# Order of the gate steps, transposes, copies and exponentials in the attention loop of a decoder layer

## What is computed

```
hn   = rmsnorm(x)
proj = hn @ w_in                      # q, k, v of two mixers, 3 head gates, and mg (2 x 1024 columns)
o_a  = banded_attention(window 128, 8 heads, sinks, bias)            # branch A
o_cmp, o_slc = compressed (63 blocks) and full causal attention      # branches C and S
o_win = banded_attention(window 512, 8 heads, bias)                  # branch W
o_b  = g0 * o_cmp + g1 * o_slc + g2 * o_win
g_a, g_b = sigmoid(mg)
h = x + (g_a * (o_a @ w_br_a) + g_b * (o_b @ w_br_b)) @ w_out
h = h + moe(rmsnorm(h))               # 32 experts, top-1 group, top-2 in it
out = rmsnorm(h)
```

## Time and profile before

| what | value |
|---|---|
| time, median of 3 runs | 1778.69 us (1776.9 to 1779.84) |
| the profiled execution, its own time | 1784.23 us |
| its span | 1782.4 us |
| granted clock over the span | 0.954 |
| PE busy | 1557.8 us (87%) |
| DVE busy | 537.1 us (30%) |
| ACT busy | 348.3 us (20%) |
| POOL busy | 262.8 us (15%) |

### The profile page before, as it was taken

How to read it: one execution, slowest core, us unless ns; L and a number is a source line. 1 busy time by engine, 2 the same in 40 slices (tenths; PEclk the granted TensorE clock), 3 DMA queues, 4 the chain that set the end, 5 groups by cost and what they waited for, 6 DMA issues and landing times.

```text
span 1782.4 us, 20856 instructions
## 1 busy us (share of the span) xinstructions
PE 1557.8 (87%) x7526; PEld 828.0 (46%) x7527; DVE 537.1 (30%) x1378; ACT 348.3 (20%) x859; POOL 262.8 (15%) x363
## 2 busy tenths in 40 slices
PE   6999998989989898988999994199799999889990
PEld 3554543434444444443444552156355666446650
DVE  4210005665565545553222215011011111101116
ACT  3000003343433433342000111011011111111112
POOL 2000002333232232221000000300000000000003
PEclk9999999999999999998999997599899999999995
DMA  9124602443111111002536410979999999999967
GB/s 254 26 59 57 132 0 100 166 142 95 30 33 34 30 24 42 25 18 77 204 115 232 172 53 18 341 283 380 383 389 384 379 391 381 391 390 383 381 223 283
DMA packets 130215, 334.21 MB, mean 188 GB/s; under 512 B 36792, under 2 KB 72664, under 8 KB 120944
## 3 DMA queue, kind: packets, MB, share of 16 engines
q1 hardware_dynamic: 112208, 291.88, 46.8%
q0 software_dynamic: 9552, 29.55, 5.0%
q10 hardware_dynamic: 8400, 12.07, 1.9%
HBM read 276.06 MB, written 57.41 MB: 187 GB/s over the span
## 4 chain that ended last, share of the span: by engine, by line
PE 71%; DMA 9%; DVE 8%; SPq 6%; issue 3%; ACT 2%; POOL 2%; ACTq 0%; POOLq 0%; DVEq 0%
PE PS L741 13%; PE PS L642 10%; PE PS L531 10%; PE PS L755 7%; PE PS L704 6%; PE PS L673 5%; SPq L301 5%; PE PS L628 4%; PE PS L589 4%; PE PS L608 3%; PE PS L526 2%; DMA BA<-w 2%; DMA WA<-w 2%; DMA BA<-rows_d 2%; DVE mx L1022 1%
## 5 line engine op out<-in xcount | busy, mean ns | idle before, releaser
L642 PE MATMUL PS<-WA 128*128 128x512 f32 x512 | 260.3, 621 | 17.8 <-ACT WA L833 17.8
L741 PE MATMUL PS<-WA,BA 128*64 128x256 f32 x2048 | 235.8, 388 | 14.1 <-DMA WA<-w 12.9
L741 PEld LDWEIGHTS PS<-WA,BA 128*64 128x64 f32 x2048 | 172.9, 140 | 84.6 <-issue 22.1
L531 PE MATMUL PS<-WA,BA 128*128 128x512 f32 x416 | 183.1, 601 | 5.1 <-DVE WA L937 5.1
L1248 POOL TENSOR_SCALAR BA<-BA,rin,gates 128x640 f32<-128x640 f32 (+7 forms) x128 | 99.8, 780 | 301.8 <-DVE rin L1045 301.7
L1161 DVE SCALAR_TENSOR_TENSOR BA<-BA,PS 128x256 f32<-128x256 f32 x46 | 19.4, 421 | 408.4 <-ACT BA L880 408.4
L642 PEld LDWEIGHTS PS<-WA 128*128 128x128 f32 x512 | 85.6, 191 | 111.5 <-issue 80.9
L826 ACT ACTIVATE BA<-PS,ngm 128x640 f32<-128x640 f32 (+7 forms) x128 | 89.7, 701 | 218.2 <-DVE ngm L1023 218.0
L531 PEld LDWEIGHTS PS<-WA,BA 128*128 128x128 f32 x416 | 79.6, 193 | 103.9 <-issue 98.3
L755 PE MATMUL PS<-WA,BA 128*64 128x512 f32 x512 | 116.9, 597 | 11.7 <-DVE BA L1171 7.6
L1287 POOL DMA_DIRECT2D BA<-rows_d x92 | 48.1, 522 | 531.1 <-PE PS L722 528.1
(11 more groups left out here) (207 smaller groups left out, 1361.4 us busy)
## 6 DMA issues: line engine op xcount, KB each, us to landing
WA<-w SPq DMA_DIRECT2D x66, 2048.0 KB, 34.4
BA<-w SPq DMA_DIRECT2D x30, 2048.0 KB, 36.7
rows_d<-WA SPq DMA_DIRECT2D x7, 2048.0 KB, 7.5
BA<-rows_d POOLq DMA_DIRECT2D x94, 128.0 KB, 7.2
rows_d<-BA ACTq DMA_DIRECT2D x92, 128.0 KB, 7.8
WA<-w_in SPq DMA_DIRECT2D x16, 512.0 KB, 5.5
gates_d<-WA SPq DMA_DIRECT2D x32, 256.0 KB, 2.2
WA<-gates_d SPq DMA_DIRECT2D x8, 1024.0 KB, 6.0
```

The source lines that it names most:

```text
L531: mm = pe.matmul(PS[:, j % 4, :], ws[:, c % 6, k, :], hnT[:, k, 512 * h:512 * h + 512], start=(k == 0), stop=(k == KT - 1))
L642: mm = pe.matmul(PS[:, 6, :], gw[:, j, k, :], hnT[:, k, 512 * hf:512 * hf + 512], start=(k == 0), stop=(k == KT - 1))
L741: mm = pe.matmul(PS[DH * h:DH * h + DH, bank, 0:256], xT[:, k, :], w[par][:, k, 256 * h:256 * h + 256], start=(k == 0), stop=(k == KT - 1))
```

## The change

On PE the transposes and the values of a turn of the loop now come directly behind its scores, and its gate steps behind those. On ACT a turn with a trailing unit keeps the order exponential, copies; in a turn with a leading unit (A and C among them) the copies of n - 2 come ahead of the exponential. The tanh of a gate tile is the last thing of a turn, behind the move of the sums. No instruction is added or removed; DVE, POOL and SP keep their orders. The lines in the changed kernel are moved by 3 on PE (L608 is L611, L642 is L645) and otherwise on ACT.

```diff
+    def leads(n):
+        return units[n][1] in "AC" or units[n][2] < REP
...
         for n in range(NU + 3):
             if n < NU:
-                if units[n][1] in "AC" or units[n][2] < REP:
+                if leads(n):
                     scores(n)
-                for step in steps_at[n]:
-                    gate_step(step)
             if 2 <= n < NU + 2:
                 turn(n - 2)
             if n >= 3 and (n - 3) == last_of[units[n - 3][:2]]:
                 values(*units[n - 3][:2])
+            if n < NU:
+                for step in steps_at[n]:
+                    gate_step(step)
...
         for n in range(NU + 3):
-            if n < NU:
-                i, br, h, kbs = units[n]
-                ...
-                last.then_inc(S["exp_done"], 1)
-                for m in tile_done_at.get(n, ()):
-                    ...
+            if n < NU and not leads(n):
+                exponential(n)
             if 2 <= n < NU + 2:
-                for m in range(first_group[n - 2], first_group[n - 1]):
-                    if m % 2 == 0:
-                        move_group(m)
+                move_groups(n - 2)
+            if n < NU and leads(n):
+                exponential(n)
             if n >= 3 and (n - 3) == last_of[units[n - 3][:2]]:
...
+            for m in tile_done_at.get(n, ()):
+                act.wait_ge(S["gate_in"], m + 1)
+                if m >= 2:
+                    act.wait_ge(S[f"gst{m % 2}"], 16 * (m // 2))
+                nc.scalar.activation(gst[:, m % 2, :], PS[:, 6, :], ACT.Tanh, scale=0.5).then_inc(S["gate_act"], 1)
```

More of the change, by code:

```diff
@@ L804, in move_group @@
             last.then_inc(S["evac_act"], 1)
-        for n in range(NU + 3):
-            if n < NU:
-                i, br, h, kbs = units[n]
[L810 to L827, removed]
-                last.then_inc(S["exp_done"], 1)
-                for m in tile_done_at.get(n, ()):
[L830 to L833, removed]
@@ new lines, in exponential @@
+        def exponential(n):
+            i, br, h, kbs = units[n]
+            act.wait_ge(S["front"], n + 1)
+            if n >= 3:
+                act.wait_ge(S["t_done"], first_group[n - 2])
+            nk = P * len(kbs)
+            s0, v = 2 * (n % 2), n % 4
+            if br == "A":
+                nc.scalar.activation(esk[:, v, :], esk[:, v, :], ACT.Exp)
+                for g in range(2):
+                    last = nc.scalar.activation(PB[:, n % 3, nk * g:nk * g + nk], PS[:, s0 + g, 0:nk],
+                                                ACT.Exp, bias=ngm[:, v, g:g + 1], scale=SC,
+                                                accum_out=den[:, v, g:g + 1])
+            elif br == "C":
+                last = nc.scalar.activation(pc[:, :, :], pc[:, :, :], ACT.Exp, scale=SC)
+            else:
+                src = PS[:, s0:s0 + 2, :].rearrange("p a n -> p (a n)")[:, 0:nk]
+                last = nc.scalar.activation(PB[:, n % 3, 0:nk], src, ACT.Exp, bias=ngm[:, v, 0:1], scale=SC,
+                                            accum_out=den[:, v, 0:1])
+            last.then_inc(S["exp_done"], 1)
@@ L834, in _, with move_groups @@
+        def move_groups(u):
+            for m in range(first_group[u], first_group[u + 1]):
+                if m % 2 == 0:
+                    move_group(m)
+        for n in range(NU + 3):
+            if n < NU and not leads(n):
+                exponential(n)
             if 2 <= n < NU + 2:
-                for m in range(first_group[n - 2], first_group[n - 1]):
-                    if m % 2 == 0:
-                        move_group(m)
+                move_groups(n - 2)
+            if n < NU and leads(n):
+                exponential(n)
```

## The result

The changed kernel takes 1801.52 us in the median of 4 runs (1796.86 to 1809.83); the kernel before, run beside it, 1779.26 us (4 runs, 1776.9 to 1780.88). The ratio is 1.0131 (95% interval 1.0086 to 1.0177): slower by some 22 us. The forecast was 1787.6, slower by 8.9: the direction held, the size did not, and the time lies above the range.

A forecast was written before the change was run, and what follows sets the result against it. The prediction took the attention loop, a ring of PE, DVE, ACT and POOL, as the bound. Pairs -10.9, A/C +16.4 and clock +3.4 gave +8.9 us on 1778.69: 1787.6, range 1775 to 1799.

The forecast's parts named there:

- A/C: Stretch of four units A, unit C and first pair W per query block: loses +16.4 us, PE waiting for POOL.
- The sum: Working added up over the loop's stretches: -10.9 + 16.4 + 3.4 = +8.9 us.
- now two gate steps first, 13.7: Block 4: two gate steps ahead of the fourth unit A's scores, which start at 13.7 us instead of 12.0.
- Pairs: The other seven pairs of each query block: win -10.9 us, about 3.4 of it two falls of the clock.
- The rule for a pair: Each pair follows engine-ring latency, POOL plus transposes plus trailing steps, or PE's work; examples 6.31 and 5.74 us.
- rival 1: Faster: trailing transposes in pairs do not really wait for POOL; -6 us, 1773, chance 0.17.
- The clock: Granted clock's falls in the loop counted as two, as before: 3.4 us come back; bounds none and 13.6.
- Rival 2: Slower by the clock: falls at unit C of every block, +18 to +22 us, 1797 to 1801, chance 0.18.
- ACT, counted at nothing: ACT's copies ahead of a leading exponential cost nothing where transposes lie directly behind scores; up to 0.3 us at unit C.
- Tanh waits gone: In the loop, PE's 17.8 us of gate steps waiting on the tanh nearly go.
- DVE's 0.81 wait gone: In pairs, DVE's wait of 0.81 us ahead of the leading copy goes.
- waits on POOL grown to some 30: PE's waits on POOL at the transposes, 3.6 us for A before, grow to some 30 us.

The follow-up runs named there:

- e9: Kernel before (old order), with POOL's scaling of the units A cut to one column of each group: 1796.82 us.
- e10: Changed kernel (new order), with the same cut of POOL's scaling of the units A to one column of each group: 1813.47 us.
- e12: Changed kernel with the 13 gate steps at the third unit A put back ahead of transposes and values: 1787.16 us, ratio 1.0043.
- e4: Against the kernel before, gate steps late and ACT's copies early only in leading units of the second to eighth pairs: 1769.11 us, ratio 0.9950.
- e8: Changed kernel with one or two matmuls of zeros ahead of transposes that wait for POOL, at the third unit A and unit C: 1790.76 us, ratio 1.0070.
- the repeat: Changed kernel once more, no edit, for a second profile and the spread of times: 1800.13 us, ratio 1.0130.
- e5: New order only in the second to eighth pairs of each query block, old order in units A, C and first pair W: 1777.05 us, ratio 0.9989.
- e7: e4 with gate steps also behind the transposes in trailing units whose leading unit ended a gate tile: 1766.34 us, ratio 0.9931.
- e2: Only PE's part of the change, ACT keeping its old order: 1803.66 us, ratio 1.0136.
- e3: Only ACT's part of the change, PE keeping its old order: 1797.95 us, ratio 1.0100.

## Why the prediction was right in direction and wrong in size

**A/C, right.** The sum forecast +16.4. Measured +23.5, of which four falls of the clock are 6.8: +16.7 from the order. Block 4 follows the working step by step. Counted from 499.30, the fourth unit's scores start at 15.48, and without the 1.7 of the fall at 13.8 (forecast 13.7); the pair W at 22.28, without the same 1.7 at 20.6 (20.6); the next scores at 532.38 - 499.30 = 33.08, without 3.4 at 29.7 (30.1). The reason that I gave, stands behind POOL, was only part of it: the thin scaling (e9, e10) took most of A's stands away and left 16.7 of 22 us, and the 13 steps of e12, between values and scores, made 7.4 us of the 16.7. My laying out had both in it ("now two gate steps first, 13.7"), so the number held. Which part each of the other places has in the remaining 9.3 us was not tested.

**Pairs, too much won.** Forecast -10.9, of it -3.4 for two falls that go. Measured -5.3, with those two falls gone: the order won 1.9, not 7.5. This is one of the two terms that failed, by 5.6 us. The rule for a pair was right (6.38 for 6.31, 5.81 for 5.74), but 0.07 short each time; if every pair had that, it would be about 4 us over 56 pairs. The rows show where: the next gate step starts 573.57 - 572.97 = 0.60 us behind the first of five transposes and 467.30 - 466.81 = 0.49 behind the first of four, where the sum had 0.54 and 0.43. The sum's values came from transposes that stood directly behind gate steps. It is not the wait that makes the difference: transposes directly behind scores, without a wait, take 0.60 and 0.49 too (464.37 to 464.86 in the pair W shown). Another part lies in the first inner pair, which carries unit C's values: in block 4 it took 7.2 us, where the sum had 6.5. The seven pairs of block 4 took 581.75 - 532.38 = 49.4 us, forecast 48.4. That each trailing transposes' wait for POOL would eat the gain was right against rival 1, and e4 shows what it was worth: with trailing steps ahead, 5.96 us.

**The clock, the other term that failed.** I counted two falls as before. The two of the pairs did go; in A/C, where there had been none, came four in one profile and six in another, which had a seventh in the pairs. That is 6.8 to 11.9 us where the sum had 3.4, and filling the stands (e8) won 9.4 us of the time. Rival 2 had the mechanism and nearly the time (1797 to 1801), with 0.18, and its place, unit C's transposes, was one of three. In after the fall of block 7 is there, behind a stand of 2.24 us, while the longer one of block 5 brought none:

```profile
608.08 0.66 PE L611 MATMUL PS<-ident,pc 128*128 128x128 f32 x4 [2.48 <-POOL pc L1257]
608.67 1.94 PE L631 MATMUL PS<-BA 128*64 128x512 f32 x8
...
779.39 0.65 PE L611 MATMUL PS<-ident,pc 128*128 128x128 f32 x4 [2.24 <-POOL pc L1257]
779.98 3.06 PE L631 MATMUL PS<-BA 128*64 128x512 f32 x8
```

1.94 us for those eight is full clock, 3.06 is not. In the repeat it is block 5 that falls. The other places in after are the third unit A, in blocks 3 and 4, and the scores of the first pair W, in block 4. I had weighed that one gap of 1.39 us had brought no fall; one gap without a fall says little of many longer ones, and in e5 and e7, with the old order in A/C, the same gap (1.39 and 1.38 us) did bring one.

**The sum against the median.** Order 16.7 - 1.9 = 14.8, falls +3.4 more than before: 18.2 in the two profiles. The medians are 22.3 apart, and the forecast had 8.9, all of it order, so 13.4 us are missing from it: 5.9 of order, nearly all in the pairs, and some 7.5 of clock. The clock on record bears that out for all executions: without what they lost to it the kernels are 15.5 us apart, and the changed one lost 7.1 us more. The two profiled ones show less of it because they differ by only two falls in the loop.

**ACT, counted at nothing.** Right as far as "costs nothing behind early transposes" goes, but not a part that could be left out: e2 and e3 show it worth 7 us in the pairs with PE's part and harmful without. "Tanh waits gone" was right (0.8), "DVE's 0.81 wait gone" too, "waits on POOL grown to some 30" was 58.9: I had forgotten that a wait can grow and the path not.

**What stays open.** Which of the stands brings a fall: two profiles of the same kernel, with the same stands, have falls in different blocks. The stand of 2.48 us at unit C of block 5 brought one in the repeat, in e8 and in e12, and none in after. And what the order costs at unit C and the first pair W.

## What to carry to other kernels

Work that may go anywhere (here the gate steps) belongs where an engine has to wait in any case, ahead of the instruction that waits, and not between the end of one link of a latency chain and the start of the next. Where the order of one engine is turned, the engine that takes its results should be turned with it: half of such a change can be as bad as the whole. Price a new stand of PE twice, once as idle time and once for the clock that may fall behind it, and where the clock is at stake, try filling the stand with matmuls on zeros before anything else.

## What the runs showed of the hardware

Added work made the kernel faster, twice: matmuls on zeros in stands of 1 to 2 us gave 9.4 us (1800.13 to 1790.76), seven of them in the tail some 6 (1766.34 to 1760.36, ratio 0.9931 to 0.9895). Stands of about 2 us with only transposes behind could be followed by half clock: behind the stand of 2.03 us and 0.66 us of transposes, the values ran at 5.30 instead of 3.65 us. They need not be: the stand of 2.48 us at unit C of block 5 had a fall behind it in one execution of the changed kernel and none in another. Five transposes took 0.54 us directly behind gate steps, and 0.60 behind scores or behind a wait. And one kernel's executions differ in how much clock they lose: 75 to 92 us of some 1800 over eight executions of the changed kernel, 68 to 73 over six with the stands filled.
